# Moving two operand pairs by 8 bytes per partition in a two-block decoder kernel

## The reference, cut to what matters

```python
for l in range(DEPTH):                       # first block
    h = rms_norm(x, g_mix[l])
    proj = h @ w_in[l]                       # 1024 -> 10052 columns, split into ten parts
    ...                                      # y_a, y_b, y_c, y_d: four branches, each @ its w_o
    gates = jax.nn.sigmoid(gate_in + b_gate[l]).reshape(bsz, seq, N_BRANCH, dm)
    merged = gates[:, :, 0] * y_a + gates[:, :, 1] * y_b + gates[:, :, 2] * y_c + gates[:, :, 3] * y_d
    x = x + merged @ w_merge[l]
    h2 = rms_norm(x, g_ffn[l])
    gt = causal_dwconv(h2 @ w_ffn_gate[l], ffn_conv_w[l])
    x = x + (jax.nn.silu(gt) * (h2 @ w_ffn_up[l])) @ w_ffn_down[l]
for l in range(DEPTH):                       # second block
    h = rmsnorm(x, norm_w[l])
    proj = h @ w_in[l]
    ...
    x = x + concatenate([y_mla, y_gdn, y_moba]) @ w_out[l]
return rmsnorm(x, final_norm_w)
```

## Time and profile before

| | |
|---|---|
| Time, median of 2 runs | 1373.95 us (1371.28 to 1376.62) |
| Span of the profiled execution, first to last instruction | 1369.2 us |
| PE busy | 1345.0 us, 98% of the span, 10828 matmuls |
| PEld busy | 1265.4 us, 92% |
| DVE busy | 1040.0 us, 76% |
| ACT busy | 750.9 us, 55% |
| POOL busy | 46.3 us, 3% |
| DMA | 223.77 MB, mean 163 GB/s |

### The profile page before, as it was taken

How to read it: one execution, slowest core, us unless ns; L and a number is a source line. 1 busy time by engine, 2 the same in 40 slices (tenths; PEclk the granted TensorE clock), 3 DMA queues, 4 the chain that set the end, 5 groups by cost and what they waited for, 6 DMA issues and landing times. The chain is left out here.

```text
span 1369.2 us, 26498 instructions
## 1 busy us (share of the span) xinstructions
PE 1345.0 (98%) x10828; PEld 1265.4 (92%) x10828; DVE 1040.0 (76%) x1781; ACT 750.9 (55%) x1157; POOL 46.3 (3%) x48
## 2 busy tenths in 40 slices
PE   8999999999999999999999999999999999999998
PEld 8899999998999989899999999999989899888996
DVE  6999898677766666999897767766778746777565
ACT  6544656556444455544557545544558546576363
POOL 0000000000000000000000000000000110001100
PEclk9999999999999999999999999999999999999999
DMA  8565444564665465645364555555553324353231
GB/s 289 177 207 178 131 154 160 180 215 155 197 202 185 139 230 163 215 155 185 97 204 159 187 187 172 198 185 191 178 186 124 120 64 137 100 174 109 78 102 69
DMA packets 108992, 223.77 MB, mean 163 GB/s; under 512 B 6180, under 2 KB 17700, under 8 KB 108872
## 3 DMA queue, kind: packets, MB, share of 16 engines
q1 hardware_dynamic: 106736, 219.12, 48.2%
q10 hardware_dynamic: 2136, 2.96, 0.7%
HBM read 221.01 MB, written 1.06 MB: 162 GB/s over the span
## 5 line engine op out<-in xcount | busy, mean ns | idle before, releaser
L1755 DVE TENSOR_TENSOR wlo<-ring,whi 128x1024 fp32r<-128x1024 f32 (+3 forms) x430 | 498.1, 1180 | 182.7 <-ACT whi L1173 152.7
L1173 ACT ACTIVATE whi<-ring 128x1024 fp32r<-128x1024 f32 (+3 forms) x430 | 433.2, 1026 | 361.8 <-PE bank L499 228.7
L499 PE MATMUL bank<-hhi,whi 128*128 128x256 f32 x2016 | 278.8, 280 | 6.0 <-ACT sgb L1431 3.9
L508 PE MATMUL bank<-hhi,wlo 128*128 128x256 f32 x2016 | 280.3, 281 | 0.0
L499 PE MATMUL bank<-hlo,whi 128*128 128x256 f32 x2016 | 275.3, 278 | 0.0
L499 PEld LDWEIGHTS bank<-hhi,whi 128*128 128x128 f32 x2016 | 253.1, 189 | 9.5 <-ACT sgb L1431 4.3
L508 PEld LDWEIGHTS bank<-hhi,wlo 128*128 128x128 f32 x2016 | 252.6, 189 | 3.7 <-issue 2.6
L499 PEld LDWEIGHTS bank<-hlo,whi 128*128 128x128 f32 x2016 | 251.6, 189 | 0.0
L469 PE MATMUL bank<-w 64*64 64x64 f32 (+5 forms) x1376 | 101.7, 249 | 1.5 <-DMA w<-in_flip 0.9
L1935 DVE SCALAR_TENSOR_TENSOR w<-w,par 128x256 f32<-128x256 f32 x240 | 98.0, 478 | 0.0
L521 PE MATMUL bank<-whi,hhi 128*128 128x512 f32 (+2 forms) x256 | 96.6, 379 | 0.0
(11 more groups left out here) (309 smaller groups left out, 1535.5 us busy)
## 6 DMA issues: line engine op xcount, KB each, us to landing
ring<-in_w_in SPq DMA_DIRECT2D x100, 1024.0 KB, 5.1
ring<-in_w_ffn_down SPq DMA_DIRECT2D x22, 1024.0 KB, 5.1
ring<-in_w_ffn_gate SPq DMA_DIRECT2D x20, 1024.0 KB, 5.1
ring<-in_w_ffn_up SPq DMA_DIRECT2D x20, 1024.0 KB, 5.1
ring<-in_w_merge SPq DMA_DIRECT2D x8, 1024.0 KB, 5.1
ring<-in_w_out SPq DMA_DIRECT2D x8, 1024.0 KB, 5.0
ring<-in_w_oc SPq DMA_DIRECT2D x4, 1024.0 KB, 5.3
ring<-in_w_od SPq DMA_DIRECT2D x4, 1024.0 KB, 5.2
```

Source lines behind the costliest of these rows:

```text
L499: done = e.matmul(o, wh[:, k, cols(u)], s_[:, k0 + k, :], stop=False, skip_group_check=True, start=opens and k == 0 and s_ is sh and u % 2 ...
L508: done = e.matmul(o, wl[:, k, cols(u)], sh[:, k0 + k, :], start=False, stop=closes, skip_group_check=True)
L1173: e.activation(part_of(whi, j), part_raw(j), ACT.Copy).then_inc(*up("hi.a"))
L1755: e.tensor_tensor(part_of(wlo, j), part_raw(j), part_of(whi, j), ALU.subtract).then_inc(*up("lo.v"))
```

## The change

In the kernel before, each of the four tiles is allocated with exactly its 2048 floats in a partition. In the changed kernel each is allocated with 128 floats more (2176), and the program uses the 2048 that begin at float 2, so 8 bytes further in. The added 512 bytes keep every other tile at the same place within a line of 16, 32 or 64 bytes, though at a higher address (512 bytes per enlarged tile ahead of it). `fhi` and `flo` are now declared as eight chunks instead of two by four, and `F` cuts them accordingly. The third pair, `fin`, and the weights' halves `whi` and `wlo` are not shifted.

```diff
-        hhi = sb("hhi", [P, 8, S], F32R)
-        hlo = sb("hlo", [P, 8, S], F32R)
+        def aside(ap):
+            return ap[:, 2:2 + 8 * S].rearrange("p (c s) -> p c s", s=S)
+
+        hhi = aside(sb("hhi", [P, 8 * S + 128], F32R))
+        hlo = aside(sb("hlo", [P, 8 * S + 128], F32R))
...
-        fhi = first.enter_context(nc.sbuf_tensor("fhi", [P, 2, 4, S], F32R))
-        flo = first.enter_context(nc.sbuf_tensor("flo", [P, 2, 4, S], F32R))
+        fhi = aside(first.enter_context(nc.sbuf_tensor("fhi", [P, 8 * S + 128], F32R)))
+        flo = aside(first.enter_context(nc.sbuf_tensor("flo", [P, 8 * S + 128], F32R)))
...
-        F = [(fhi[:, q], flo[:, q]) for q in range(2)]
+        F = [(fhi[:, 4 * q:4 * q + 4], flo[:, 4 * q:4 * q + 4]) for q in range(2)]
```

## The result

The changed kernel took 1405.95 us (1405.66 to 1406.23, 2 runs) against 1373.95 us; the ratio is 1.023 with a 95% interval of 1.018 to 1.0279. That the kernel became slower is clear; whether by more than 2% is not, since 2% lies inside the interval. The forecast of the likeliest case, 1374, was missed, and so was its own range of 1366 to 1390. The time lies in the stated range of 1362 to 1436, at the place of rival B (up to 1405).

The account below looks back on a forecast made before the run. The kernel was taken as a line of matmuls on PE, count times start-to-start distance. All four address costs summed to 0 on a 1369.2 us span; with 4.75 us to the runs' median the forecast was 1374, range 1362 to 1436.

Parts of the forecast that it names:

- the likeliest case: Whole kernel: the shift costs nothing, or up to one line's worth; 1374 us, own range 1366 to 1390, chance 0.56.
- rival B: Matmuls of `chans`: pace goes up a step or two, about 4 ns each; 1396 to 1436 us, chance 0.20.
- the two paces of the earlier trace: Same 256-column matmul in `chans`: 113.6 and 117.5 ns at full clock, taken as a step in the hardware, not waits.
- Item 1: Moving operand of `chans`, 6960 matmuls: a start in the middle of a 32-byte unit is free; cost taken as zero.
- one line's worth: Upper end of the no-change case for the whole kernel, whose range is 1366 to 1390 us.
- Item 2: Stationary operand of `toks` and `last_pair`: the weight load has 228 ns to hide in, could double; cost nothing.
- Items 3 and 4: ACT and DVE writes to and DVE reads of the shifted tiles: nothing more; 401, 343, 632 and 693 ns kept.
- the bubble: In `chans`: the half line at the end could put all matmuls on the slower pace, 27 to 31 us.
- Rival C: Whole kernel: a time above the stated range of 1362 to 1436 us, which leaves it out; chance 0.16.
- Rival D: Matmuls of `chans`: faster if the shift breaks what locks the slower pace; 1362 us, at the limit 1325; chance 0.08.

Follow-up runs that it names:

- the first stream: Only 256-, 512- and 128-column matmuls timed, the computation left out, 64 per stretch at stated operand offsets; 256 columns took 113.3 to 123.3 ns on the first pass.
- off16: Against the kernel before: all four pair tiles start 16 bytes in, a whole line, with the change's padding; 1399.6 us, ratio 1.0169.
- off64: Against the kernel before: the four pair tiles start 64 bytes in, the weights' halves unshifted; 1400.86 us, ratio 1.0183.
- both8: Against the kernel before: pair tiles and weights' halves all start 8 bytes in, so their distance is kept; 1412.55 us, ratio 1.0271.
- both64: Against the kernel before: pair tiles and weights' halves all start 64 bytes in, so their distance is kept; 1374.82 us, ratio 0.9998.
- off4: Against the kernel before: all four pair tiles start 4 bytes in, one float; 1412.35 us, ratio 1.0257.
- the map: Matmul-only stream, moving operand set further from the stationary one in steps of 8 bytes; first-pass means 117.8 ns on the line, 120.4 off it.
- pair176: Against the kernel before: the four pair tiles start 176 bytes in, distance 112 instead of 192 (mod 256); 1376.64 us, ratio 1.0034.
- the second pass: The same stretches of matmuls again in another order, three small matmuls ahead of each; over the distances, means 117.7 ns on the line, 120.5 off it.

## Why the prediction was right and where it failed

**What bounds the kernel: right.** Time is the matmul count times the distance of starts. PE's idle time even fell, and a change in nothing but the pace moved the end by 34.7 us of span. The prediction took the two paces of the earlier trace rows for the sign of an operand feed that is just about saturated, and this is where rival B came from. That the pace moves with the operands' addresses alone fits it; no run measures the feed itself. The time fell into the stated range by luck: the largest part of the chances stood on no change, and the part that covered 1406 had another mechanism.

**Item 1, the moving operand: wrong, and this is the step that failed.** It looked for the price only in where the operand stands within a line, and took zero. No run shows that zero; in its place the runs put 120.4 ns instead of 114.7 per matmul, 34.5 us in the trace. It said a start in the middle of a 32-byte unit is free, from the equal starts of the earlier trace rows. That row couldn't carry it: there the moving operand is 324 columns of weights and the pair is stationary, and for 256 columns the first stream put +0, +16, +32 and +64 bytes, all on a line, at 120.0, 116.7, 116.7 and 113.3 ns. What was missing is the other operand. The pace hangs on how the stationary and the moving operand lie to each other. off16 and off64, both on the line, lose 23.4 and 25.2 us, where the change loses 32.0. In the profile weight loads run beside the matmuls (PEld is busy for 1265.4 us of a span of 1369.2 and PE for 1345.0), so the two reads may get in each other's way; that is the author's guess and not shown, since no run streams without weight loads.

Half a line has a price too: 2.6 ns on average over the distances, and 5 to 6 ns at the kernel's own (121.0 in both8 against 114.7 before and 115.8 in both64). No run shows the one line's worth that the likeliest case's range allows for; in its place stand these prices, and 38 us for `chans` in both8. The price of the half line holds on average and not for each place: at +12 bytes the stream took 116.7 ns, less than the 120.0 at +0. The stationary operand's place counts as well: with float32r operands, moving the stationary tile alone by 64 bytes takes the stream from 120.0 to 113.8 ns (in one of five stretches to 117.8), and off64 against both64 makes 26 us of such a shift in the kernel.

**Item 2, the stationary operand in `toks`: nearly right.** The timeline of the changed kernel, beside the earlier trace rows:

```profile
48.62 1.09 PE L532 MATMUL bank<-wlo,hhi 128*128 128x512 f32 x4
49.55 0.39 PE L524 MATMUL bank<-whi,hhi 128*128 128x512 f32 x1
```

Four matmuls of 512 columns take 0.93 us where they took 0.91. Over the whole traces the step is smaller: the mean from start to start with 512 columns goes from 229.1 to 230.7 ns on the shifted pairs, 2.2 us in all 1488, and stays at 229.4 and 229.3 on `fin`, the unshifted pair that the prediction named as the control. The cover of the weight load wasn't what decided here either, but the distance: off64 gives 227.1 ns, less than before.

**Items 3 and 4, ACT and DVE: right.** 402, 344, 633 and 693 ns, within 1 ns of the 401, 343, 632 and 693 named.

**Rival B: right in size, wrong in mechanism.** It gave up to 1405 us by one step of 4 ns for all. The step is to 120.0 ns, above the old slow pace. No run shows the bubble from which B took its step. The half line does have a price, as B said, but it isn't a lock on the slower of the old paces, and the distance alone is enough for most of the step (off16 and off64, 23.4 and 25.2 of 32.0 us). That the two came to the size that B named is luck. B's chance, 0.20, should have been larger: the two paces of one and the same matmul showed that more than the byte count sets the rate, and every distance other than the present one was unmeasured. **Rival C** (0.16), a time above the stated range, didn't come: the change costs 32.0 us, and off4, one float in, 36. **Rival D** didn't come; the map has no distance below 113.3 ns, and the kernel before stands at one of the two best.

## What to carry to other kernels

In this kernel PE runs float32r matmuls back to back at full clock, and the addresses of the two operands alone moved their mean pace between 114.0 and 121.1 ns. Where a kernel is bound like this, treat them as a tuning parameter: read the distance between starts, not durations, and compare it over a few placements, because a shift that looks neutral (16 or 64 bytes, still aligned) cost 1.7 and 1.8% here. Put a control that keeps the relation beside every alignment test; both64 against off64 said in two runs what no single shift could. Measure both roles of a tile, since what helps it as the moving operand can hurt it as the stationary one (pair176: 3 us gained, 6 lost).

## What the runs showed of the hardware that was not expected

- The pace of a 256-column float32r matmul, weight load beside it, ranged from 113.3 to 123.3 ns with the operands' addresses and the order of the stretches alone. At 512 columns it ranged from 227 to 237 ns; at 128 columns, with +0 and +8 bytes, it stayed at 111 to 112, and plain float32 stayed at 216 to 217 for each of its two.
- The map over the distance is narrow and uneven: 113.8 ns at 192, 114.5 at 112, and 118.6 to 119.8 at their neighbours 16 bytes away (208 gave 116.7 on the second pass). Half a line off, at 200 and 120, both dips are gone (120.0 and 121.3 ns). Shifts of the moving operand by 256 and by 512 bytes gave the same 120.0 and 119.8. What makes the pattern no run shows.
- Two steady paces, 113.3 and 117.8 ns, occur at distances that are 64 or 192 mod 256, the kernel's own among them. They are the two paces of the kernel before (113.6 ns in the earlier trace rows, 117.5 in the earlier trace rows). A shift of the moving operand by 192 gave 113.3 in every stretch of the streams, one by 704 gave 117.8 in every stretch, and one by 64, 448 or 960 gave both. What selects one is open: the same distance changed its pace with what ran before it. In the kernel before, 68% of the starts in `chans` are at most 115 ns apart, so little is left to gain there: the mean is 114.7 ns against 113.3.
